# The delta rule's scan of a two-block model on one core: whole-array products, half-zero corrected values, a second state buffer

## The reference, cut to what matters

```python
def _gated_deltanet(q, k, v, alpha, beta, a_log, dt_bias):
    ...
    u_t, w = sol[..., :A_DV], sol[..., A_DV:]
    p_intra = jnp.einsum("bhncd,bhnjd->bhncj", q, k) * decay
    q_dec = q * jnp.exp(G)[..., None]
    g_last = G[..., -1]
    k_dec = k * jnp.exp(g_last[..., None] - G)[..., None]
    ...
    def step(S, inp):
        ut, wt, pt, qt, kt, et = inp
        U = ut - jnp.einsum("bhck,bhkv->bhcv", wt, S)
        o = jnp.einsum("bhck,bhkv->bhcv", qt, S) + jnp.einsum("bhcj,bhjv->bhcv", pt, U)
        S = S * et[..., None, None] + jnp.einsum("bhck,bhcv->bhkv", kt, U)
        return S, o

    S0 = jnp.zeros((b, A_HEADS, A_DK, A_DV), f32)
    _, o = lax.scan(step, S0, xs)
```

## Time and profile before

| | us |
|---|---|
| median of 3 runs | 2709.15 |
| lowest and highest | 2704.40 and 2710.46 |
| the profiled execution, its own time | 2707.19 |
| its span, first to last instruction | 2705.9 |
| TensorE busy in the span | 2603.8 (96%) |
| VectorE, ScalarE, GpSimd busy | 1086.9, 954.0, 1185.3 |
| mean granted TensorE clock | 0.984 |
| first and last product of the scan | 1375.0 and 1771.2 |

### The profile page before, as it was taken

The page is one execution under the profiler, slowest core; times in us unless marked ns, Lnnn a source line. Parts: engine busy times, 40 slices in busy tenths (PEclk is TensorE's granted clock), DMA queues, the critical chain, the costliest instruction groups (busy, mean ns, idle before and its releaser), DMA issues.

```text
span 2705.9 us, 32969 instructions
## 1 busy us (share of the span) xinstructions
PE 2603.8 (96%) x12952; PEld 2117.8 (78%) x12952; DVE 1086.9 (40%) x2298; ACT 954.0 (35%) x1444; POOL 1185.3 (44%) x1572
## 2 busy tenths in 40 slices
PE   7999999999999999998999999999998999999997
PEld 5777888887778888877878788777876887888886
DVE  7964111126863111147646663323345523311112
ACT  4453222233543222235433242324454433322222
POOL 2115655641136656644323132343333554565653
PEclk9999999999999999999999999999999999999998
DMA  5532223237423223241101010113221231223222
GB/s 185 135 98 82 105 86 109 84 103 179 102 86 108 85 97 108 76 143 63 47 32 47 32 48 32 47 63 117 86 78 66 106 125 63 94 91 105 94 90 74
DMA packets 41803, 241.50 MB, mean 89 GB/s; under 512 B 4657, under 2 KB 5809, under 8 KB 18481
## 3 DMA queue, kind: packets, MB, share of 16 engines
q1 hardware_dynamic: 38768, 218.43, 23.2%
q0 software_dynamic: 2880, 20.97, 3.8%
HBM read 214.21 MB, written 4.19 MB: 81 GB/s over the span
## 4 chain that ended last, share of the span: by engine, by line
PE 82%; DVE 11%; ACT 2%; POOL 2%; issue 2%; DMA 1%; SPq 0%; DVEq 0%; ACTq 0%; POOLq 0%
PE PB L1724 65%; PE PB L1762 4%; PE PB L1726 3%; POOL WL L2755 2%; DVE cc L2385 2%; ACT WH L1984 1%; PE PB L1908 1%; PE PB L1939 1%; PE PB L1905 1%; PE PB L1920 1%; PE PB L1736 1%; DVE pa L2459 1%; PE PB L1927 1%; PE PB L1744 1%; PE PB L1886 1%
## 5 line engine op out<-in xcount | busy, mean ns | idle before, releaser
L2755 POOL TENSOR_TENSOR WL<-WR,WH 128x256 fp32r<-128x256 f32 x1412 | 1013.1, 753 | 781.7 <-ACT WH L1984 781.7
L1724 PE MATMUL PB<-HH,WH 128*128 128x512 f32 x1992 | 804.9, 404 | 11.9 <-ACT HH L1999 8.9
L1724 PE MATMUL PB<-HL,WH 128*128 128x512 f32 x1992 | 785.6, 394 | 3.4 <-DVE HL L2282 3.3
L1724 PE MATMUL PB<-HH,WL 128*128 128x512 f32 x1992 | 523.8, 398 | 9.5 <-DMA WL<-WR 6.8
L1984 ACT ACTIVATE WH<-WR 128x2048 fp32r<-128x2048 f32 (+1 forms) x209 | 371.6, 1778 | 260.3 <-PE PB L1724 256.1
L1724 PEld LDWEIGHTS PB<-HH,WH 128*128 128x128 f32 x1992 | 378.2, 190 | 105.8 <-issue 16.4
L1724 PEld LDWEIGHTS PB<-HL,WH 128*128 128x128 f32 x1992 | 378.2, 190 | 85.6 <-DVE HL L2282 8.9
L1724 PEld LDWEIGHTS PB<-HH,WL 128*128 128x128 f32 x1992 | 367.2, 189 | 89.0 <-DMA WL<-WR 7.6
L1724 PE MATMUL PB<-BL,WH 128*128 128x512 f32 x848 | 333.9, 394 | 0.8 <-DVE BL L2291 0.8
L1724 PE MATMUL PB<-BH,WH 128*128 128x512 f32 x784 | 309.6, 395 | 2.7 <-ACT BH L2013 2.7
L1724 PE MATMUL PB<-BH,WL 128*128 128x512 f32 x784 | 197.5, 396 | 7.1 <-POOL WL L2755 7.1
(11 more groups left out here) (345 smaller groups left out, 3105.4 us busy)
## 6 DMA issues: line engine op xcount, KB each, us to landing
WR<-in_w_gu SPq DMA_DIRECT2D x66, 1024.0 KB, 4.8
WR<-in_w_dn SPq DMA_DIRECT2D x48, 704.0 KB, 4.0
WR<-in_w_in SPq DMA_DIRECT2D x22, 1024.0 KB, 4.9
WL<-WR POOLq DMA_DIRECT2D x20, 1024.0 KB, 7.0
WR<-in_qkv SPq DMA_DIRECT2D x12, 1024.0 KB, 4.8
WR<-in_w_out SPq DMA_DIRECT2D x8, 1024.0 KB, 4.8
WR<-in_qk SPq DMA_DIRECT2D x8, 1024.0 KB, 4.9
WR<-in_gb SPq DMA_DIRECT2D x4, 1024.0 KB, 4.8
```

What stands on the lines that cost most here:

```text
L1724: ins = pe.matmul(out[:, 0:n], wt[:, k * cols + j * P:k * cols + (j + 1) * P], x[:, k, 0:n], start=first, stop=last)
L2755: ins = g.tensor_tensor(m.WL[u % 2][:, part], m.WR[u % 2][:, part], f32(m.WH[u % 2][:, part]), ALU.subtract)
```

## The change

Every product of the scan now takes the whole array:

- c1 takes the 128 columns of WT of the whole block of two chunks, and writes 128 rows of PSUM; VectorE reads only the chunk's 64 rows of it, as before.
- UU becomes two buffers. Even chunks use the first, whose rows 64 to 127 are zero; odd chunks the second, whose rows 0 to 63 are zero. c2 and the second product of c3 then run over all 128 rows. The two zero halves are written once by two memsets ahead of the first group's c0, with a wait for them.
- SS becomes two buffers. c4 reads the state of its chunk and writes the other buffer. It waits for c3 of the chunk before (through `sfree`), no longer for c3 of its own.
- The second buffers take the place of the causal mask; a few constants move by six columns, so that they begin on 32 bytes. CON has 2312 columns in place of 2306.

```diff
-C_ID, C_ONE, C_INVF, C_SGN, C_SWAP, C_CAUS, C_INCL, C_LEV, C_RST = 0, 128, 256, 257, 258, 386, 898, 1026, 1794
-NCON = 2306
+C_ID, C_ONE, C_INVF, C_SGN, C_SWAP, C_CAUS, C_INCL, C_LEV, C_RST = 0, 128, 256, 257, 264, 392, 904, 1032, 1800
+NCON = 2312
...
-    m.O, m.UU, m.SS, m.RC, m.l2c, m.zc = (t[n] for n in ("O", "UU", "SS", "RC", "l2c", "zc"))
+    m.O, m.RC, m.l2c, m.zc = (t[n] for n in ("O", "RC", "l2c", "zc"))
+    causal = con_off + 4 * C_CAUS
+    m.UU, m.SS = ([t[n], at(n + "1", [P, 2, P], causal + 1024 * i, F32, con_off + 4 * C_INCL)[0]] for i, n in enumerate(("UU", "SS")))
...
-        sfree = {"S": f, "U": f}
+        sfree = [f, f]
...
-            step("c0", gi, after=sfree["S"])
+            step("c0", gi, after=sfree[0] + sfree[1])
...
-                pe("c1", gi, n, tile=t1, after=sfree["U"])
+                pe("c1", gi, n, tile=t1, after=sfree[n % 2])
...
-                sfree["U"] = sfree["S"] = [done]
                 if n < 7:
-                    step("c4", gi, n, tile=t3, done=done)
+                    step("c4", gi, n, tile=t3, after=sfree[(n + 1) % 2])
                     room3.free(at("c4", gi, n))
+                sfree[n % 2] = [done]
...
-                ins = pe.matmul(PB[t.b][rows, i * P:i * P + P], m.WT[g][:, i, 64 * n:64 * n + 64], m.SS[:, i, :], start=True, stop=True)
+                ins = pe.matmul(PB[t.b][:, i * P:i * P + P], m.WT[g][:, i, bl * P:(bl + 1) * P], m.SS[n % 2][:, i, :], start=True, stop=True)
...
-                ins = pe.matmul(PB[t.b][:, i * P:i * P + P], m.KD[g][rows, i, bl * P:(bl + 1) * P], m.UU[rows, i, :], start=True, stop=True)
+                ins = pe.matmul(PB[t.b][:, i * P:i * P + P], m.KD[g][:, i, bl * P:(bl + 1) * P], m.UU[n % 2][:, i, :], start=True, stop=True)
...
-                pe.matmul(PB[t.b][:, oc], m.SS[:, i, :], m.QD[g][:, i, 64 * n:64 * n + 64], start=True, stop=False)
+                pe.matmul(PB[t.b][:, oc], m.SS[n % 2][:, i, :], m.QD[g][:, i, 64 * n:64 * n + 64], start=True, stop=False)
...
-                ins = pe.matmul(PB[t.b][:, oc], m.UU[rows, i, :], m.PT[g][rows, i, bl * P + r0:bl * P + r0 + 64], start=False, stop=True)
+                ins = pe.matmul(PB[t.b][:, oc], m.UU[n % 2][:, i, :], m.PT[g][:, i, bl * P + r0:bl * P + r0 + 64], start=False, stop=True)
...
             ve.all(w["after"])
-            v.memset(m.SS[:], 0.0).then_inc(sems["c0"], 1)
+            if key[0] == 0:
+                for n in range(2):
+                    dv.link(v.memset(m.UU[n][64 - 64 * n:128 - 64 * n, :, :], 0.0))
+                dv.wait()
+            v.memset(m.SS[0][:], 0.0).then_inc(sems["c0"], 1)
...
-            v.tensor_tensor(m.UU[rows, :, :], m.UT[gi % 2][rows, :, bl * P:(bl + 1) * P],
+            v.tensor_tensor(m.UU[n % 2][rows, :, :], m.UT[gi % 2][rows, :, bl * P:(bl + 1) * P],
                             PB[w["tile"].b][rows, 0:256].rearrange("p (h q) -> p h q", q=P), ALU.subtract).then_inc(sems["c1u"], 1)
...
             ve.wait_ge(*w["tile"].done)
-            ve.wait_ge(*w["done"])
+            ve.all(w["after"])
             ve.wait_ge(*at("pel", 2 * gi + 1))
+            old, new = m.SS[n % 2], m.SS[(n + 1) % 2]
             for i in range(2):
-                ins = v.scalar_tensor_tensor(m.SS[:, i, :], m.SS[:, i, :], m.EL[gi % 2][:, i, n:n + 1], blk(PB[w["tile"].b], i), ALU.mult, ALU.add)
+                ins = v.scalar_tensor_tensor(new[:, i, :], old[:, i, :], m.EL[gi % 2][:, i, n:n + 1], blk(PB[w["tile"].b], i), ALU.mult, ALU.add)
```

More of the change, by code:

```diff
@@ L120, in memory @@
     m.WL = [sb(f"WL{i}", [P, 2048], F32R) for i in range(2)]
+    con_off = cur[0]
     m.CON = sb("CON", [P, NCON])
@@ L1880, in tensor_program @@
             gi, n = key
-            g, t, rows = gi % 2, w["tile"], slice(64 * (n % 2), 64 * (n % 2) + 64)
+            g, t, bl = gi % 2, w["tile"], n // 2
             te.all(t.after)
@@ L1889, in tensor_program @@
             gi, n = key
-            g, t, rows, bl = gi % 2, w["tile"], slice(64 * (n % 2), 64 * (n % 2) + 64), n // 2
+            g, t, bl = gi % 2, w["tile"], n // 2
             te.all(t.after)
@@ L1899, in tensor_program @@
             g, t, r0, bl = gi % 2, w["tile"], 64 * (n % 2), n // 2
-            rows = slice(r0, r0 + 64)
             te.all(t.after)
```

## The result

| | before | after |
|---|---|---|
| median, us | 2708.28 (4 runs) | 2676.86 (4 runs) |
| lowest and highest, us | 2704.40 and 2710.46 | 2674.61 and 2679.24 |
| span of the profiled execution, us | 2705.9 | 2673.3 |
| first product of the scan to the last, us | 396.1 | 365.0 |

The ratio is 0.9892, with a 95% interval from 0.9878 to 0.9906: 29 us faster, between 25 and 33. Forecast were 36 us and 2671 us, with a range from 2662 to 2688 us.

A forecast was written before the change was run, and what follows sets the result against it. TensorE's list of instructions was taken to bound the kernel. Terms 39.1 - 0.8 - 3 + 1.2 - 0.6 gave 36 us saved, from 2707.2 us to 2671 us, range 2662 to 2688 us.

The forecast's parts named there:

- Whole-array products: Scan products c1, c2, c3: removing 248 switches between parts of the array, some 0.16 us each, saves 39.1 us.
- entries behind a wait: Five entries into c1 or c2 follow a wait on VectorE, so their hidden drains, 0.8 us, are not gained.
- Wider c1: c1's loads grow from 64 to 128 columns but lie under the product ahead: no cost, 7.0 us if uncovered.
- The rival of open loads: c2 and half of c3: 240 whole-array passes lose their load overlap, 27 us back, run at 2698 us; chance 0.03.
- Waits that open: TensorE's waits shortly behind scan products: ten may each take back two switches, 0.32 us, together 3 us lost.
- The rival of latency: Scan products as shorter filler: TensorE waits for YY, MM or UU, up to half lost, 2687 us; chance 0.11.
- its sign: In the scan stretch, waits on YY, MM, UU or SS summing to over 20 us would show latency.
- Second state buffer: c4 waits only for c2, so VectorE's state update ends about a microsecond earlier relative to TensorE: 1.2 us gained.
- Memsets: Two more memsets and a wait, once, in front of the first c1: 0.6 us lost, bounds 0.3 and 0.8.
- Order: Planner's clocks stay, so the same list of steps is expected, with nothing new in any queue but the memsets.
- Constants: Six more columns in the first DMA, moved masks keep their readers' shapes: 0, bounds plus or minus 1 us.

The follow-up runs named there:

- the mirrored order: Kernel before with only c3's four products reordered to UU, SS of the first head, then SS, UU of the second: 2699.13 us, ratio 0.9970.
- the one that gave 15 us: Kernel before with only c3's order changed, both UU products first, then both SS products: 2693.29 us, ratio 0.9945.

## Why the prediction was right, and where its sum was off

1. **Whole-array products.** Forecast 39.1 us less 0.8 us for entries behind a wait, 38.3; measured 37.6 in the gaps. The price of a switch, worked out from two stretches as 0.158 us, held within some 0.02 us in every profile. That c3 behind whole-array products starts without extra was the row that decided it.
2. **Wider c1.** Forecast nil; four loads of 128 columns fit into 0.45 us of products. The rival of open loads (its 240 x 0.11 is 26 us, not 27) is out: whole-array passes in the scan follow each other every 0.11 us with loads of 0.19 us. The rule of the Trainium skill that stood beside it (TensorE: Matmul & The Clock Gate, Part 3: Packing small matmuls) does not describe these loads.
3. **Waits that open.** This is the term of the sum that was mis-sized. With terms 4 and 5 the forecast for everything away from the switches was -3 + 1.2 - 0.6, a loss of 2.4 us; these distances lost 6.5. Most of it is the waits on YY: 1.3 us before, 5.3 after, where the sum had 0.3 us for each wait. I counted two switches of lead for each wait; but leads add up along a run of chunks, and a queue that TensorE used to meet late enough is then met too early. That leads add up is argued from the one place shown above, not tried by a run. The rival of latency names the right mechanism, at a third of its price; its sign, over 20 us of waits on YY, MM, UU and SS, was not reached (15.5 us).
4. **Second state buffer.** Forecast 1.2 us of gain; there is none. The wait for SS came from VectorE's queue. The step "TensorE waited for them once, 1.6 us; I take 1.2 us of gain" took the instruction that the wait names for its cause, and did not ask what had held that instruction.
5. **Memsets.** Forecast 0.6 us; the waits for c0's memset went from 3.7 to 4.5 us, 0.8.
6. **Order.** As forecast, the same products in the same order.
7. **Constants.** Forecast nil within 1 us, "Readers of the moved masks (POOL's L2779 and others) keep their shapes". This is the step that failed: the masks' place costs some 7 to 9 us on the kernel before by the two kernels that move it, and some 5 to 12 on the changed one. With the constants at their old places the run is at 2671 us, the number forecast. That agreement is partly luck: terms 3 to 5 were 4 us too favourable, and the granted clock, which I left alone, gave something back.

The range held, and it needed its width: the profile of before showed the masks at one place only, so the bound of 1 us on term 7 had nothing behind it.

## What to carry to other kernels

When TensorE bounds a stretch, compare the starts of its instructions, not its busy share: 248 changes between parts of the array hid 38 us in a row that read 96% busy. Either fill the operands with zeros and take the whole array, which cost no time in a pass here, or, without any memory, order products so that those on the same part stand together, as far as the sums in PSUM allow: the mirrored order gave 8 us and right sums, the one that gave 15 us did not keep them. And when a change moves a buffer or a table, count that as a part of the change of its own: look at the minimum duration of each instruction that reads it, and try its move alone.

## What the runs showed of the hardware that was not expected

- A float32 product of GpSimd, 128x512 with a mask of 128 columns read four times over, took 1.10 us with the mask at byte 8 or 24 of 64 from the start of its table, and 1.28 us at byte 16 or 32. Other places were not tried.
- Some 0.19 us more per mask, 32 times, came with a lower mean granted clock of TensorE, 0.982 against 0.986, and with 7 to 9 us of run time. Multiplied by its mean clock, each run of the kernel before in these sessions comes to 2664 to 2671 us, each run of the two kernels with moved masks to 2663 to 2669, and each run of the change to 2634 to 2639: beside the clock nothing of the masks' cost is left, and the scatter of one kernel's runs is almost wholly the clock's.
- A change from one part of the array to another cost about 0.15 us in float32 work (0.146 to 0.150 at the full clock, 0.138 to 0.161 over all profiles), in two parts, one ahead of the first pass and one ahead of the second. Changes to and from 128x64 (0.160 us) and 64x128 (0.155 us) were priced alike here.
